# A decoder block in one kernel: x loaded ahead of the weights, an exponential moved behind the input norm, and two u tiles multiplied in token halves

## The reference

```
hn    = rmsnorm(x, mix_norm_pre)            # 512 x 1024
proj  = hn @ w_in                           # c_q, c_kv, k_r, u (512 columns), gates
dt    = exp(log_dt)                         # step sizes of the state-space layer
mag   = exp(lr * dt);  ang = li * dt        # its decay and angle, per group and state
a     = mag * (cos ang, sin ang); z = (a - 1) / lambda; bb = z * b
s     = scan over tokens of a*s + bb*u;  y = c*s + d*u;  y = gelu(y); y *= sigmoid(y @ w_glu + b)
attn  = causal attention of 8 heads from c_q, c_kv, k_r
x     = x + rmsnorm((gate0 * attn @ Wa + gate1 * y @ Ws) @ w_out, ...)
x     = x + rmsnorm(conv_ffn(rmsnorm(x, ...)), ...)
```

## Time and profile before

| | |
|---|---|
| three runs | 871.37, 867.49 and 872.58 us (median 871.37) |
| span of the profiled execution | 871.9 us |
| TensorE busy | 767.0 us (88%), 3450 matmuls |
| VectorE busy | 462.9 us (53%) |
| GpSimd busy | 565.6 us (65%) |
| ScalarE busy | 280.4 us (32%) |

### The profile page before, as it was taken

How to read it: one execution, slowest core, us unless ns; L and a number is a source line. 1 busy time by engine, 2 the same in 40 slices (tenths; PEclk the granted TensorE clock), 3 DMA queues, 4 the chain that set the end, 5 groups by cost and what they waited for, 6 DMA issues and landing times.

```text
span 871.9 us, 11494 instructions
## 1 busy us (share of the span) xinstructions
PE 767.0 (88%) x3450; PEld 635.6 (73%) x3450; DVE 462.9 (53%) x767; ACT 280.4 (32%) x570; POOL 565.6 (65%) x727
## 2 busy tenths in 40 slices
PE   2993948898898989789999399999999999999995
PEld 2782826687876777668777388888888888888884
DVE  6899998888874665755501723333333334211115
ACT  4172316368565454541102411111111112111113
POOL 5572876368254244258866677777777778798881
PEclk9896968787778999989999599999999999999998
DMA  7131111001035123016332133333333333343322
GB/s 262 49 97 49 48 49 48 25 25 48 25 73 133 37 64 94 27 60 229 97 85 73 44 101 97 97 96 96 96 96 96 96 96 96 85 108 96 96 73 96
DMA packets 37823, 73.22 MB, mean 84 GB/s; under 512 B 4512, under 2 KB 4768, under 8 KB 37792
## 3 DMA queue, kind: packets, MB, share of 16 engines
q1 hardware_dynamic: 36064, 66.54, 26.5%
q10 hardware_dynamic: 1728, 6.29, 2.0%
HBM read 67.57 MB, written 2.10 MB: 80 GB/s over the span
## 4 chain that ended last, share of the span: by engine, by line
PE 67%; DVE 22%; ACT 4%; issue 4%; POOL 1%; DMA 1%; SPq 1%; POOLq 0%; DVEq 0%; ACTq 0%
PE ps L518 22%; PE ps L520 21%; PE ps L519 21%; DVE u_lo L1431 2%; DVE bt L1325 1%; DVE pT_lo L1646 1%; DVE small L1266 1%; PE ps L632 1%; DVE small L1325 1%; DVE xn L1702 1%; DVE small L1269 1%; DVE r_bc L1548 1%; ACT y_f L1054 1%; DVE prob L1659 1%; DVE small L1263 1%
## 5 line engine op out<-in xcount | busy, mean ns | idle before, releaser
L472 POOL TENSOR_TENSOR w_lo<-raw,w_hi 128x512 fp32r<-128x512 f32 x230 | 320.3, 1393 | 19.2
L518 PE MATMUL ps<-xT_hi,w_hi 128*128 128x512 f32 x560 | 229.1, 409 | 21.0 <-DVE u_lo L1431 14.3
L469 POOL TENSOR_TENSOR w_hi<-raw,ones 128x1 fp32r<-128x1 f32 x230 | 60.0, 261 | 254.1 <-PE ps L520 237.0
L519 PE MATMUL ps<-xT_lo,w_hi 128*128 128x512 f32 x560 | 223.9, 400 | 0.0
L520 PE MATMUL ps<-xT_hi,w_lo 128*128 128x512 f32 x560 | 223.3, 399 | 0.0
L470 POOL TENSOR_SCALAR w_hi<-raw 128x511 fp32r<-128x511 f32 x230 | 153.4, 667 | 0.1
L518 PEld LDWEIGHTS ps<-xT_hi,w_hi 128*128 128x128 f32 x560 | 109.5, 196 | 44.6 <-DVE u_lo L1431 14.7
L520 PEld LDWEIGHTS ps<-xT_hi,w_lo 128*128 128x128 f32 x560 | 108.8, 194 | 23.7
L519 PEld LDWEIGHTS ps<-xT_lo,w_hi 128*128 128x128 f32 x560 | 109.5, 195 | 21.5
L1721 DVE SCALAR_TENSOR_TENSOR conv<-ps,vec,conv 128x511 f32<-128x511 f32 x44 | 33.0, 749 | 144.1 <-ACT conv L1217 144.1
L1217 ACT ACTIVATE conv<-ps,vec 128x512 f32<-128x512 f32 x44 | 34.3, 781 | 195.6 <-PE ps L520 195.6
(11 more groups left out here) (260 smaller groups left out, 1318.3 us busy)
## 6 DMA issues: line engine op xcount, KB each, us to landing
raw<-in_w_stream_dram SPq DMA_DIRECT2D x230, 256.0 KB, 2.6
x_in<-in_x_dram ACTq DMA_DIRECT2D x4, 512.0 KB, 8.7
q_hl<-qr_hl SPq DMA_DIRECT2D x16, 128.0 KB, 2.3
x<-in_x_dram ACTq DMA_DIRECT2D x4, 512.0 KB, 4.8
out_dram<-x SPq DMA_DIRECT2D x4, 512.0 KB, 2.6
k_hl<-kr_hl SPq DMA_DIRECT2D x4, 256.0 KB, 4.1
g_mix_pre<-in_norms_dram ACTq DMA_DIRECT2D x1, 512.0 KB, 6.1
bc_in<-in_ssm_bc_dram SPq DMA_DIRECT2D x1, 512.0 KB, 10.4
```

The costliest lines, as they stand in the source:

```text
L469: pool.tensor_tensor(w_hi[:, s, 0:1], raw[:, s, 0:1], ones[:, 0:1], ALU.mult)
L472: pool.tensor_tensor(w_lo[:, s, :], raw[:, s, :], w_hi[:, s, :].bitcast(F32), ALU.subtract).then_inc(weights_split, 1)
L518: pe.matmul(o, wh, xh, start=start, stop=False, skip_group_check=True)
L519: pe.matmul(o, wh, xl, start=False, stop=False, skip_group_check=True)
```

## The change

It has three parts. The gain `g_mix_pre` is issued by SyncE ahead of everything, no longer by ScalarE behind the first x tile, and SyncE waits for the second x tile (`x_landed[1]`) before it issues the first four weight chunks and what stands behind them. The exponential of the step size moves in VectorE's list from ahead of the norm to behind the last `split_xT`. TensorE multiplies u tiles 0 and 1 in two halves of 256 tokens: the first half of tile 0 stands between the third and the fourth transpose, the first half of tile 1 behind the fourth.

```diff
@@ SyncE
+            sp.dma_start(g_mix_pre[:, :], norms[0:1, :].partition_broadcast(P).rearrange("p a d -> p (a d)")).then_inc(g_landed, 16)
             sp.dma_start(small[:, 0:3, :], ssm_small).then_inc(small_landed, 16)
+            sp.wait_ge(x_landed[1], 16)
             for s in range(RING):
                 load(s, s)
@@ TensorE
             pe.wait_ge(consts_ready, 5)
-            for t in range(TT):
+            def first_half(j, half):
+                cols = slice(half * L // 2, (half + 1) * L // 2)
+                for part in range(2):
+                    c = FIRST[("u", j)] + part
+                    s = c % RING
+                    pe.wait_ge(weights_split, c + 1)
+                    for k in range(4):
+                        last = three(ps[:, j, cols], w_hi[:, s, k * P:(k + 1) * P], w_lo[:, s, k * P:(k + 1) * P],
+                                     xT_hi[:, 4 * part + k, cols], xT_lo[:, 4 * part + k, cols],
+                                     part == 0 and k == 0, part == 1 and k == 3)
+                    if half == 1:
+                        last.then_inc(chunks_multiplied, 1)
+
+            for t in range(TT - 1):
                 transpose_x(PRE + t)
-
+            pe.wait_ge(xT_split, TT)
+            first_half(0, 0)
+            transpose_x(PRE + TT - 1)
+            first_half(1, 0)
             pe.wait_ge(xT_split, 2 * TT)
-            for j in range(NU):
+            first_half(0, 1)
+            first_half(1, 1)
+            for j in range(2, NU):
                 in_tile(("u", j), j)
@@ ScalarE
             for t in range(TT):
                 act.dma_start(x_in[:, t, :], x_t[t, :, :]).then_inc(x_landed[t], 16)
-                if t == 0:
-                    act.dma_start(g_mix_pre[:, :], norms[0:1, :].partition_broadcast(P).rearrange("p a d -> p (a d)")).then_inc(g_landed, 16)
@@ VectorE
-            dve.wait_ge(small_landed, 16)
-            exponential(sm("dt"), sm("ldt"))
-
             for t in range(TT):
                 rsqrt_mean(PRE + t, D)
...
             split_xT(TT - 1)
+            dve.wait_ge(small_landed, 16)
+            exponential(sm("dt"), sm("ldt"))
             tt(sm("ang"), sm("li"), sm("dt"), ALU.mult)
```

## The result

The changed kernel takes 877.31 us in the median of six runs (876.68 to 878.94), the kernel before 871.29 (867.49 to 873.41, six runs). The ratio is 1.0076, with a 95% interval of 1.0050 to 1.0102: slower by 6.0 us, where 4.0 was forecast (875.4, range 869 to 880). The profiled execution took 878.94 us, 1.8 more than its span of 877.1.

The account below looks back on a forecast made before the run. VectorE's list up to the first `u_lo` was taken as the bound; an earlier norm, given back by held-back transposes, plus 3.8 us of exponential in series put `ang` 4.0 us later, giving 875.4 us against the median, range 869 to 880.

Parts of the forecast that it names:

- The path: VectorE's full list up to the first `u_lo` sets the time; a shift at 25 us passes to the end one for one.
- The exponential, 3.8 us: Behind the norm in VectorE's list, its 18 instructions stand in series before `ang`: 3.8 us, upper bound 5.6.
- the 55.5 that I had named as a sign: VectorE from `ang` to the first `u_lo` takes about 55.5 us; otherwise the prediction is wrong.
- the number of splits beside the list: GpSimd's later chunks stretch VectorE's list as before, with the same number of splits beside it: nothing added.
- The norm's start: First square at 4.9 us, first `xn` at 8.0 instead of 10.20; the last `xn` ends 2.2 us earlier.
- which I gave 0.3 us: At the first loads, queues take equal turns, so x tile 0 lands near 5.2: the sum would be 0.3 us more.
- The held-back transposes: On TensorE, 24 half-width products from 17.5 take 4.3 us, the fourth transposes 1.5, ending at 23.3 instead of 23.17.
- The sum: `ang` at 29.0 instead of 25.04, 4.0 us later; 871.9 + 4.0 = 875.9 profiled, 875.4 against the median.
- TensorE's wait for `u_lo`: TensorE's front comes 2 to 3 us earlier, ahead of its 14.3 us wait, which grows to about 20.
- Full clock through the half: TensorE at full clock through transposes and first half; fourth transpose waits 1 us at most: +0.7 to +2.5 us, chance 0.22.
- the third case: Slow clock throughout, and GpSimd beside the exponential or chunk 1 late: +5.5 to +9 us, 877 to 880, chance 0.23.
- The fourth: Faster because GpSimd's splits stretch VectorE's list less; eight of sixteen meetings saved, 8.4 us, would give 867; chance 0.1.

Follow-up runs that it names:

- the paced kernel: The kernel before with one added wait: TensorE holds the c_q tiles until VectorE's list reaches the `bt` products; 864.13 us, ratio 0.9907.
- f_weights_wait: The kernel before with the weight loads alone waiting for the second x tile, behind the load of `small`; ratio 0.9975, median moved by -1.1 us.
- d_exp_last_only: The kernel before with only the step-size exponential moved behind the norm; 874.05 us, ratio 1.0033.
- b_transposes_first: The changed kernel with all four transposes ahead of the first half of tile 0; 874.84 us, ratio 1.0051 against the kernel before.
- m_after_again: The changed kernel, unchanged, timed once more beside the last group; 879.77 us, ratio 1.0086 against the kernel before.
- i_more_tensore: The kernel before with 48 more matmuls of 512 columns in front of u tiles 0 and 1, output unchanged; ratio 0.9934, 5.7 us faster.

## Why the prediction was nearly right

**The path.** That VectorE's list sets the first 80 us is shown: each term that I took away or added alone moved `u_lo`, and the median followed with the same sign. That a shift is passed to the end one for one, as I had put it, is not: by the medians the changed kernel lost 1.9 and 3.0 us more than `u_lo` moved, the paced kernel kept 7.8 of its 11.9 us, and where `u_lo` stood still (f_weights_wait) the median moved by 1.1 us.

**The exponential, 3.8 us.** Confirmed three times (3.76, 3.76, 3.75) where GpSimd did not run beside it. In the changed kernel it took 5.5: this term of the sum was too small by 1.7 us. The forecast had GpSimd's chunk 4 starting at about 28, it started at 28.03, and I had put `ang` at 29.0, a contradiction of 1 us in my own text. One cast took 1.15 us (29.11 to 30.26) beside GpSimd's

```profile
28.91 1.31 POOL L474 TENSOR_TENSOR w_lo<-raw,w_hi 128x512 fp32r<-128x512 f32 x1
```

So `ang` came at 31.02 and not at 29.0, and from `ang` to `u_lo` it took 53.6 us and not the 55.5 that I had named as a sign. The two are one thing: the splits that met the exponential were missing behind it, and the stretching adds up to some 21 us in both kernels. Errors of +2.0 and -1.9 us thus cancel in the 4.1 us at `u_lo`. I had added nothing for the number of splits beside the list, and that was right; that they would meet the exponential I had not seen.

**The norm's start.** This step failed in size: "I let the first square start at 4.9". It started at 6.39. The recurrence behind it was right (9.6 us from the first to the last `xn`, 9.7 forecast), so the lead of the norm was 1.0 us at the last `xn`, not 2.2. A small slip stands in the sum as well: square and readout take 1.17 us (4.87 to 6.04), not 1.25. The Trainium skill's page "DMA: Bandwidth & Descriptors" (section "Queues, rings and completion order"), by which queues take turns packet by packet and which I gave 0.3 us, has the direction right. The rows show more: before, ScalarE's queue had moved 0.52 MB by 4 us and SyncE's 0.04, so x tile 0 had had the engines to itself; my 3.8 us was the price of an empty machine.

**The held-back transposes.** The sum of the 24 products (4.3, measured 4.2) and the pass from slow to full clock within them were right; the start was 0.9 late (18.41 against 17.5) behind the late norm, and the fourth transposes took 1.04 us instead of the 1.5 that I allowed. The end, 23.64, was forecast at 23.3. Three errors of +0.9, -0.1 and -0.5 us nearly cancel, which is luck.

**The sum.** I had taken the span of before for the profiled execution's time; since a run takes some 1.8 us more than its span, that execution stood further above the median than the 0.5 I wrote. Only the difference was carried over, so the forecast doesn't hang on it. At `u_lo`, 4.0 us were forecast and 4.1 measured, of which, in the order exponential, loads with halves behind the transposes, hold, +1.9, +0.7 and +1.5 (d_exp_last_only; from it to b_transposes_first; from that to the changed kernel); the middle one is smaller than the scatter of the landmarks. The path and the sign were right; that the number agrees so closely is luck. The medians are +6.0 and +7.8. Alone, the three parts moved the median by 2.6, 2.5 and 1.8 us, 6.9 together. TensorE's wait for `u_lo` was forecast at about 20 us and was 24.6, as TensorE arrived 6.2 us earlier and not 2 to 3; it lies ahead of the wait and changes nothing.

**What stays open.** By the medians the changed kernel loses 2 to 3 us more than `u_lo` moved. The stretch from the first product of w_out to the end is nearly the same in the profiles in which I read it (401.2 to 401.3 us in five). The scatter lies mostly between 171 and 476 us. Three kernels there, from the first product of the scan to w_out: before, changed and b_transposes_first.

```profile
171.47:470.69 299.22, 270.86 (x1303) 229.55 (x1303) 178.39 (x290) 130.69 (x286) 164.25 (x204) 0.91 0.27 77
```
```profile
175.24:475.87 300.63, 272.36 (x1304) 230.93 (x1304) 177.93 (x290) 132.01 (x287) 163.45 (x204) 0.91 0.26 77
```
```profile
174.18:466.82 292.64, 263.20 (x1304) 222.80 (x1304) 175.60 (x290) 130.69 (x287) 166.44 (x204) 0.94 0.27 79
```

The same work takes 8 us less where the granted clock is 0.94 and not 0.91. The profiled b_transposes_first (869.86 us) fell on the short side of its runs (869.86 to 878.91), so this is a matter of the single execution. The mean granted clock of whole runs lies at 0.919 to 0.928 in the twelve of the changed kernel and at 0.922 to 0.939 in the 81 of the kernel before, where 0.01 less goes with 4 to 6 us more. But part of that difference comes from the longer wait for `u_lo` itself, in whose last part the clock is low (0.57 in the 9.62 us behind 84.65), and that costs nothing. Whether the changed kernel meets the slow level more often in its busy stages, or something else costs the 2 to 3 us, stays open.

**The rivals.** Full clock through the half did not happen. Of the third case one half came true, GpSimd beside the exponential, and the other, the slow clock throughout, did not, though m_after_again came nearer to it (third transposes slow, products 0.21 us apart up to 21.7). Its range, 877 to 880, is where the medians fell: `ang` was late by 6.0 us, as it has it, but `u_lo` by 4.1 only, and the rest came behind. The fourth, fewer meetings with splits, is a live mechanism and the largest in this stage, worth 5.7 to 9.5 us by the medians where it was used. The change does not trigger it, as forecast: 16 splits in both.

## What to carry over

Where VectorE's list is the bound and GpSimd works beside it, look at what runs beside what, before moving instructions: pacing the producer of GpSimd's work with one semaphore gave 7.8 us, and the change of this study lost 6.0 and 7.8. A term that is stretched in one place is often relieved in another, so follow the sum to the landmark that TensorE waits for. A transfer's time read in an empty machine isn't its time once another queue starts at the same instant; and whoever pulls work into a gap of TensorE should ask what stands in order behind it, and at which clock both would run.

## What I had not expected of the hardware

- A split of 128x512 on GpSimd costs VectorE 1.27 to 1.55 us while VectorE works within SBUF, and nothing measurable in `u_lo` and `xT_lo`, which read PSUM. Every stretched instruction on 128x16 ends with one of GpSimd's, within 0.07 us, as if it had been held until then. The page "GPSIMD Engine Reference" of the Trainium skill (its table of specifications) speaks of contention with VectorE instructions that have two SBUF inputs or a two-port mode; the runs agree for two SBUF inputs and add the price. Casts and copies with one input were stretched as well (1.15 us); in which mode they ran, the trace does not show.
- 48 more matmuls, and in another kernel a wait of 11.9 us, made the program faster by 5.7 and 7.8 us.
- Products of 256 columns are 0.12 us apart at the full clock and 0.21 at half, those of 128 columns 0.11 and 0.21.
- Single executions of one kernel lie up to 10 us apart (before, in 35 runs on one chip: 866.53 to 876.82), and the stage from the scan to w_out ran at granted clocks of 0.90 (302.8 us, i_more_tensore) to 0.94 (292.6, b_transposes_first).
